# Delta rule's triangular inverse in 64x64 squares for tile 0, in whole width for tiles 1 and 2, with a new order on every engine

## What is computed

```python
kb = kc * bc[..., None]
lmat = jnp.where(strict, jnp.einsum('nbhid,nbhjd->nbhij', kb, kc) * decay, 0.0)
tmat = lax.linalg.triangular_solve(eye + lmat, eye, left_side=True, lower=True, unit_diagonal=True)
u = jnp.einsum('nbhij,nbhjd->nbhid', tmat, vc * bc[..., None])
```

```python
act = jnp.einsum('td,nd->tn', hf, expert_u)
a_sel = jnp.take_along_axis(act, eidx, axis=1)
coef = gates * jax.nn.gelu(a_sel, approximate=False)
dense = zeros.at[arange(T)[:, None], eidx].add(coef)
return dense @ expert_v
```

## Time and profile before

| | us |
|---|---|
| median of 3 runs | 1343.29 |
| lowest, highest | 1337.94, 1347.5 |
| the profiled execution | 1348.83 |
| its span (first to last instruction) | 1347.0 |
| granted TensorE clock, mean share | 0.861 |

### The profile page before, as it was taken

The page is one execution under the profiler, slowest core; times in us unless marked ns, Lnnn a source line. Parts: engine busy times, 40 slices in busy tenths (PEclk is TensorE's granted clock), DMA queues, the critical chain, the costliest instruction groups (busy, mean ns, idle before and its releaser), DMA issues.

```text
span 1347.0 us, 16598 instructions
## 1 busy us (share of the span) xinstructions
PE 902.6 (67%) x5942; PEld 510.0 (38%) x5942; DVE 859.9 (64%) x2283; ACT 265.2 (20%) x704; POOL 621.5 (46%) x660
## 2 busy tenths in 40 slices
PE   5896989979859877677860166001555877777775
PEld 2754668845525565354460022000112322322222
DVE  1624328899985598926199793898007766666565
ACT  3552414431314431304000001001001002000000
POOL 0010003236577556646667777776773433333330
PEclk9897989999969988889795578555787999999999
DMA  9664457999999789899999999999999999999995
GB/s 391 249 250 189 188 203 290 346 393 330 375 388 408 294 351 406 345 374 413 385 396 410 412 410 410 410 411 390 376 412 405 427 424 426 425 425 425 423 425 210
DMA packets 102305, 492.38 MB, mean 366 GB/s; under 512 B 11344, under 2 KB 12368, under 8 KB 80848
## 3 DMA queue, kind: packets, MB, share of 16 engines
q0 software_dynamic: 92624, 404.27, 75.0%
q1 hardware_dynamic: 9600, 87.05, 16.3%
HBM read 488.65 MB, written 2.62 MB: 365 GB/s over the span
## 4 chain that ended last, share of the span: by engine, by line
PE 35%; DMA 26%; DVE 20%; POOL 8%; issue 7%; ACT 4%; SPq 0%; DVEq 0%; POOLq 0%; ACTq 0%
PE bank L1202 32%; DMA big<-in_euv,consts 11%; DVE big L2033 9%; POOL big L800 6%; DMA wring<-in_euv,consts 5%; DMA wring<-in_wch 3%; DMA big<-in_ev,rowT 2%; DVE extra L2033 2%; PE bank L1222 1%; PE bank L1208 1%; DMA big<-in_eu,idx 1%; DVE wring L2033 1%; DMA extra<-in_eu,consts 1%; POOL extra L800 1%; DMA big<-in_eu,consts 1%
## 5 line engine op out<-in xcount | busy, mean ns | idle before, releaser
L1202 PE MATMUL bank<-big,W 128*32 128x512 f32 (+1 forms) x988 | 283.1, 725 | 103.0 <-DMA big<-in_ev,rowT 44.4
L2033 DVE CUSTOM_DVE_ANT_0 big<-big,hnow 128x1024 f32<-128x1024 f32 x240 | 284.7, 1217 | 103.3 <-DMA big<-in_euv,consts 51.5
L800 POOL DMA_INDIRECT big<-in_ev,rowT x171 | 163.2, 954 | 79.1 <-issue 59.2
L1202 PEld LDWEIGHTS bank<-big,W 128*32 128x32 f32 (+1 forms) x988 | 84.6, 148 | 258.5 <-issue 248.7
L1202 PE MATMUL bank<-hT,wring 128*128 128x128 f32 (+1 forms) x1088 | 152.4, 302 | 11.0 <-ACT hT L874 6.0
L1202 PE MATMUL bank<-wring,W 128*128 128x512 f32 (+1 forms) x352 | 126.5, 648 | 46.5 <-DVE W L2056 44.9
L1202 PEld LDWEIGHTS bank<-hT,wring 128*128 128x128 f32 x1088 | 143.6, 199 | 25.1 <-issue 12.5
L2033 DVE CUSTOM_DVE_ANT_0 wring<-wring,hnow 128x1024 f32<-128x1024 f32 x64 | 77.5, 1219 | 109.4 <-DMA wring<-in_euv,consts 109.2
L810 POOL DMA_INDIRECT big<-in_euv,consts x76 | 71.3, 939 | 102.0 <-PE bank L1202 98.5
L1202 PE MATMUL bank<-big 32*32 32x32 f32 (+1 forms) x1952 | 86.5, 228 | 42.3 <-issue 10.5
L789 POOL DMA_INDIRECT big<-in_eu,consts x102 | 96.6, 947 | 37.5 <-issue 24.4
(11 more groups left out here) (318 smaller groups left out, 1395.8 us busy)
## 6 DMA issues: line engine op xcount, KB each, us to landing
wring<-in_wch SPq DMA_DIRECT2D x32, 2048.0 KB, 10.8
big<-in_wch SPq DMA_DIRECT2D x6, 1536.0 KB, 9.3
tok<-in_wch SPq DMA_DIRECT2D x6, 512.0 KB, 10.4
big<-in_ev,rowT POOLq DMA_INDIRECT x171, 8.7
big<-in_eu,consts POOLq DMA_INDIRECT x102, 10.4
xs<-in_x SPq DMA_DIRECT2D x1, 1536.0 KB, 7.4
out_y<-xs SPq DMA_DIRECT2D x3, 512.0 KB, 7.8
big<-in_euv,consts POOLq DMA_INDIRECT x76, 17.8
```

Of the source, the lines that this page charges most:

```text
L800: nc.gpsimd.indirect_dma_start(row(slot), None, ev, bass.IndirectOffsetOnAxis(ap=rowT[t][:, n:n + 1], axis=0)).then_inc(rows_in[slot], 16)
L1202: return nc.tensor.matmul(out, lhsT, rhs, start=first, stop=last)
L2033: V.tensor_tensor_reduce(u, u, hnow[:, :], 1.0, 0.0, ALU.mult, ALU.add, coef[t % 2][:, n:n + 1]).then_inc(dot_ready, 1)
```

## The change

1. **Tile 0, levels 0 to 4** (`pi == 0`): `per_block` now makes two matmuls per head with a 64x64 stationary piece of a full-width matrix and 32 compact moving columns: 8 matmuls, 16 MATMUL records, instead of 16 and 32. L is masked to its 32x32 squares once (`LTB`). P comes out in compact form, DVE masks it and spreads it to 512 columns in one instruction (`in_blocks`). PE then forms TT (not T), DVE transposes it straight from PSUM to T, ACT copies TT. Level 0 is a product with a folded identity (`fold`, 32 more columns of constants), a mask and a transpose.
2. **Tiles 1 and 2**: all levels in whole width. Level 0 is one mask on 512 columns, 4 transposes on PE and one ACT copy. Levels 1 to 4 become what levels 5 and 6 were: 4 + 4 + 4 matmuls of 128x128, a mask on 512 columns, two ACT copies of 512 columns. The DVE transposes and `dn_full` are gone there.
3. **`grow` is gone**; the gate rows are made in `sq`, and each writer of `sq` waits, once, for the product that read the gate row (`sq_free`: in `rope`, `gate_rows`, `lam_step`, `head_norm`, `resid`, `take`). The masks grow from 960 to 1984 columns of 16 bits, 256 KB more to load.
4. **New lists** for all four engines. SP's list, the places of the rows and the order of the gathers among themselves are as before.

The core of the diff; the first `dn_t` is PE's, the second ACT's.

```diff
             def per_block(job, l, r):
                 for h in range(4):
                     c = slice(h * SB, (h + 1) * SB)
-                    for i in range(P // SB):
-                        q = slice(i * SB, (i + 1) * SB)
-                        ins = mm(b[q, c], l[q, c], r[q, c])
+                    for o in range(0, P, TB):
+                        q = slice(o, o + TB)
+                        ins = mm(b[q, c], l[q, h * P + o:h * P + o + TB], r[q, c] if r is not fold else r[q, :])
...
             def dn_p(t, d, lv):
-                if lv < SMALL:
-                    per_block(job, LTC[pi][d], TMC[pi][d])
+                if pi == 0 and lv < SMALL:
+                    per_block(("P", t, d, lv), LTB[pi][d], TMC[d])
                 else:
-                    per_head(job, [(LT[pi][d], TM[pi][d])])
+                    per_head(("P", t, d, lv), [(LT[pi][d], TM[pi][d])])
...
             def dn_t(t, d, lv):
-                if lv < SMALL:
-                    per_block(("T", t, d, lv), TTC[pi][d], PMC[pi][d])
+                if pi == 0 and lv < SMALL:
+                    per_block(("TT", t, d, lv), PM[pi][d], TTC[d])
                     return
                 if lv < LEVELS - 1:
                     per_head(("T", t, d, lv), [(TT[pi][d], PM[pi][d])])
...
             def dn_t(t, d, lv):
-                if lv < SMALL:
-                    evac(TMC[pi][d], ("T", t, d, lv), t_ready, ("T", t, d, lv), n=P)
+                if pi == 0 and lv < SMALL:
+                    act.wait_ge(*block_ready.at("T", t, d, lv))
+                    evac(TTC[d], ("TT", t, d, lv), t_ready, ("TT", t, d, lv), n=P)
                     return
...
             def dn_tt(t, d, lv):
-                dve.wait_ge(*t_ready.at("T", t, d, lv))
-                V.transpose(TTC[pi][d], TMC[pi][d]).then_inc(*block_ready.next("TT", t, d, lv))
+                job = ("TT", t, d, lv)
+                dve.wait_ge(*product.at(*job))
+                V.transpose(TMC[d], ps(*job)[:, 0:P]).then_inc(*block_ready.next("T", t, d, lv))
```

More of the change, by code:

```diff
@@ L188 @@
[L188 to L202, removed]
@@ new lines @@
+dn_t.0.0.3 dn_p.0.1.4 value.0.2 dn_p.0.0.4 dn_t.0.1.4 dn_t.0.0.4 mod.7 a_turn.0.3 dn_p.0.0.5 dn_p.0.1.5 dn_t.0.0.5
+dn_t.0.1.5 dn_p.0.0.6 dn_p.0.1.6 dn_t.0.0.6 dn_t.0.1.6 value.0.3 dn_v.0.0:2 dn_o.0.0:2 mod.8:10 gate.0.0.0 dn_s.0.0
+o_turn.0 gate.0.0.1 w_out.0.0 w_out_rest.0.0 w_out.0.1 w_out_rest.0.1 mod_turn.9 x_turn.1.0 dn_s.0.1 query.0.0
+query_rest.0.0 query.1.0 key_score.0.0 query_rest.1.0 channels.0.1 channels.1.1 channels.2.1 channels.3.1
+key_score.1.0 channels.4.1 c_turn.0.1 c_turn.1.1 channels.5.1 c_turn.2.1 channels.6.1 h_turn.0 channels.7.1 c_turn.3.1
@@ new lines @@
+c_turn.4.1 channels.8.1 channels.9.1 c_turn.5.1 channels.10.1 c_turn.6.1 channels.11.1 c_turn.7.1 query.2.0 c_turn.8.1
+query_rest.2.0 key_score.2.0 query.3.0 query_rest.3.0 c_turn.9.1 c_turn.10.1 c_turn.11.1 qk_turn.2 key_score.3.0
+mod.10:12 expert_rows.0.0 mod_turn.11 dn_decay.2.1 dn_scores.2.1 token.0.1:3 dn_t.2.1.0 dn_p.2.1.1 dn_t.2.1.1
+dn_p.2.1.2 dn_t.2.1.2 dn_p.2.1.3 token.2.1 dn_t.2.1.3 dn_p.2.1.4 dn_t.2.1.4 dn_p.2.1.5 qk_turn.1 dn_t.2.1.5 dn_p.2.1.6
+token.1.1 dn_t.2.1.6 token.1.2 dn_w.2.1 token.2.2 dn_v.2.1 dn_decay.1.0 dn_o.2.1 token.3.1:3 dn_scores.1.0 dn_s.2.1
@@ new lines @@
+dn_p.0.1.4 dn_p.0.0.4 dn_full.0.1 dn_full.0.0 dn_p.0.0.5 dn_p.0.1.5 dn_p.0.0.6 dn_p.0.1.6 head_norm.0.0 dn_o.0.0:2
+head_norm.0.1 gate.0.0.0 z_gate.0 dn_s.0.0 gate.0.0.1 resid.0.0:2 norm.1.0 mod_turn.9 scales.1 dn_s.0.1 top_key.0.0
+pair_sums.0.0.0 top_pair.0.0.0 places.0.0.0 chosen.0.0.0.0:2 channels.0.1 channels.1.1 experts.0.0.0 channels.2.1
+channels.3.1 top_key.1.0 channels.4.1 dot.0.0:2 channels.5.1 channels.6.1 channels.7.1 pair_sums.0.0.1 channels.8.1
+channels.9.1 channels.10.1 top_pair.0.0.1 dot.0.2:4 places.0.0.1 chosen.0.0.1.0 channels.11.1 key_norm dot.0.4
@@ new lines @@
+key_scale.2 key_scale.1 top_key.2.0 dot.0.5 chosen.0.0.1.1 dn_scale.2.1 dot.0.6 pair_sums.0.1.0 dot.0.7 experts.0.0.1
+expert_rows.0.0 dot.0.8:11 mod_turn.11 dn_decay.2.1 dot.0.11:13 dn_scores.2.1 dn_p.2.1.0 dot.0.13:15 dn_scale.1.0
+rope.1.0 top_key.3.0 dn_p.2.1.1 dot.0.15:18 dn_p.2.1.2 dot.0.18 dn_p.2.1.3 dot.0.19:26 pair_sums.0.1.1 dn_p.2.1.4
+dot.0.26:29 dn_p.2.1.5 dot.0.29:32 dn_p.2.1.6 dot.0.32:37 dn_qg.2.1 dot.0.37:45 top_pair.0.1.0 dot.0.45:48 rope.2.1
+dot.0.48:55 dn_decay.1.0 dot.0.55:59 places.0.1.0 dn_o.2.1 slot_gates.0.0 dn_scores.1.0 dn_s.2.1 chosen.0.1.0.0
@@ new lines @@
+dn_p.1.0.0 dot.0.59:63 dn_p.1.0.1 dot.0.63 coef.0.0 rope.2.0 top_pair.0.1.1 dn_scale.1.1 places.0.1.1 rope.1.1
+chosen.0.1.1.0 chosen.0.1.0.1 chosen.0.1.1.1 experts.0.1.0 dn_p.1.0.2 experts.0.1.1 slot_gates.0.1 expert_rows.0.1
+expo.1.0:2 diff.1.0 dn_p.1.0.3 dn_decay.1.1 dn_scores.1.1 dn_p.1.1.0 expo.1.2 diff.1.1 expo.1.3 diff.1.2 dn_p.1.0.4:6
+diff.1.3 dn_qg.1.1 dn_p.1.0.6 dn_p.1.1.1 dn_qg.1.0 head_norm.1.0 dn_o.1.0 dn_s.1.0 gate.0.1.0 expo.2.0 dn_scale.2.0
+dn_decay.2.0 dn_p.1.1.2 diff.2.0 dot.0.64:66 dn_scores.2.0 dot.0.66:69 dn_p.1.1.3 expo.2.1 dot.0.69 diff.2.1
```

316 lines of the change are left out of this document (159 added, 157 removed).

## The result

The changed kernel takes 1360.55 us (median of 4, 1358.06 to 1368.9) where the kernel before takes 1342.32 us beside it: ratio 1.0145, 95% interval 1.0088 to 1.0202. In a later comparison on like terms (run f1) the ratio is 1.0090, interval 1.0059 to 1.0121. So it is slower, by 12 to 18 us, where I had forecast no change. (A ratio is the comparison's own estimate and can differ from that of the medians by some 0.3%; both intervals lie above 1.) The busy times fit the edit: PE rises from 902.6 to 929.8 us, ACT from 265.2 to 283.1, DVE falls from 859.9 to 857.7. A second trace of each kernel has PE at 892.6 and 937.9 us, so a PE total is good to some 10 us.

The account below looks back on a forecast made before the run. It took DMA and POOL's gather issues plus gaps to bound the kernel behind 212 us. Terms -2.7, +2 and -3 gave -3.7 on 1348.83, 1345; less 5.5 to the median, 1340 us, range 1320 to 1364.

Parts of the forecast that it names:

- PE becomes the bound of 363 to 512 us: Rival: added PE work and longer chains delay all gathers there; +17 us, 1360 (1354 to 1372), chance 0.26.
- Stage by stage: Part pricing the delta rule of tiles 1 and 2 by pair and by POOL gap, +2 us in all.
- (1,0) and the start of (1,1): Added PE work before `v_batch.0.0.13`, PE idling 17.6 us in 363 to 400: +3 us, bounds -4 and +12.
- Gap of (1,1): POOL's 6.82 us wait at gather 160: levels 6 us longer but begun some 10 sooner: 0, bounds -5 and +10.
- the sum said +2: Tiles 1 and 2: +3 for (2,1), +3 for the batch, -4 for two thirds of the last gaps' total.
- the -3 behind 561 us: Gain from redone lists behind 561 us, not priced by rows: -3 us, bounds -6 and +6.
- PE +33 us for tiles 1 and 2: Whole-width products add 8.2 us of PE work per tile and direction, 33 for four.
- (2,1) +3, bounds 0 and 8: Stage 197 to 363 us: PE takes 8.2 us more, DVE gives 1.9 and gets `rope.2.1`; +3 us.
- Gap of the batch, +3: POOL's 9.29 us wait before 461 us for `v_batch.0.0.13` on PE grows: +3 us.
- Gap of dots, -6: POOL's 10.06 us wait before 500 us shrinks: a dot moves ahead and DVE has 3.8 us less; -6 us.
- Tile 0, -2.7: First part, up to the first gather at 212 us: fewer instruction stops, less added PE and DVE work; -2.7 us.
- The cover of 25 us at tile 1's indices: Indices ready at 635.27, used at 660.21 us: later delta rule of tiles 1 and 2 costs nothing that way.

Follow-up runs that it names:

- f1: The changed kernel unaltered, measured again beside its variants: 1355.60 us, 1.0090 of the kernel before.
- h2: Kernel before with tile 0 changed, plus whole width in tile 1's pairs (1,0) and (1,1) only, old order behind tile 0: 1360.20 us, 1.0115.
- f2: Changed kernel with the order of the kernel before behind about 545 us: 1352.10 us, 1.0060 of the kernel before.
- g1: Kernel before with tile 0 alone changed (64x64 squares, new order up to `dn_s.0.1`): 1343.68 us, 0.9986.
- g2: Changed kernel's products in all tiles, new order only up to `dn_s.0.1`, order of the kernel before behind it: 1364.90 us, 1.0169.
- g3: Changed kernel with the old order behind 545 us and whole-width products of levels 1 to 4, tiles 1 and 2, issued twice: 1378.96 us, 1.0283.
- i1: Kernel before with tile 0 alone changed, attention scores of tiles 1 and 2 issued three times: 1513.08 us, 1.0080, at the slower level.
- e2: Changed kernel with the order of the kernel before behind about 545 us, at the slower level: 1481.38 us, 0.9862 of the kernel before.
- e4: Kernel before with tile 0 alone changed (64x64 squares, new order up to `dn_s.0.1`), at the slower level: 1501.09 us, 0.9998.
- h1: Kernel before with tile 0 changed, plus whole width in the pair (2,1) only, old order behind tile 0: 1349.61 us, 1.0040.
- g4: The kernel before, unaltered, run for a second trace: 1342.45 us, one execution.
- h4: Changed kernel with each 64x64 product of tile 0 issued twice: 1362.67 us, 1.0123 of the kernel before.
- f3: Changed kernel with dots 116 to 127 ahead of `resid.2` on DVE and `s_copy.0.1` earlier on ACT: 1360.10 us, 1.0114 of the kernel before.
- f4: f3 plus an edit of PE's list, v-row batches 8 to 11 ahead of `query.0.2`: 1366.12 us, 1.0186 of the kernel before.

## Why the prediction was wrong

It said 1340 us and no change; it is 12 to 18 us slower. The wide range, 1320 to 1364, held the time only because it spanned most of the rivals too. The end that came is the one I had priced at 1360 as the rival "PE becomes the bound of 363 to 512 us".

**The step that failed** is in "Stage by stage": "(1,0) and the start of (1,1), +8.2 and +4, before `v_batch.0.0.13`: PE idles 17.6 us in 363 to 400 but mostly before its work is ready [...] +3", and "Gap of (1,1): [...] 0", with the reason against the rival, "POOL ran on until 447.15 without a stop". Whole width in tile 1 cost 17 us in the old order (h2) where these two terms said 3. The stop-free run of POOL showed only that PE was just in time: PE was busy 45.25 of 48.00 us in 400 to 448, so it had little room. The row was there; I read it as evidence for the rival and gave it 0.26. With the list that came with the change, what (2,1), the batch, the dots and (1,1) cost together is f2 against g1: 0.7%, 10 us with an interval of 5 either way, where the sum said +2. Of the miss of some 15 us (+12 in f1 for -3.7) that is 8; 6 or 7 are the -3 behind 561 us, a term without a row, where f1 less f2 is +3.5.

That more work for PE costs time is shown (g2, g3, i1). By which waits, and how much of it the longer chain of a level adds, is not. Nor does the account hold at the slower level, where whole width with the new list (e2) was faster than small squares with the old one (e4).

**Point by point.**

- *PE +33 us for tiles 1 and 2.* Right to a quarter: g2's PE total is 25.0 us above g1's (934.4 less 909.4), which differs by whole width and its steps alone. The 27.2 between the first two traces hold tile 0's part as well.
- *(2,1) +3, bounds 0 and 8.* 7 (h1, 2 to 12), inside the bounds.
- *Gap of the batch, +3.* Wrong in sign as a gap: 9.29 us at gather 131 became 0.30, with 2.81 at gather 127. The stretch from gather 64 to 127 grew all the same, from 82.1 and 80.4 us to 90.6 and 92.3. A price for one gap didn't price the stretch.
- *Gap of (1,1), 0.* 6.82 us ahead of gather 159 (5.49 in g4) became 3.67 (3.69 in f1); in the old order with whole width (g2) it stands at 6.93.
- *Gap of dots, -6.* Wrong in sign: it is 7.73 us in g4, 10.06 in the earlier trace rows, and 11.91 to 11.96 in the traces of the changed kernel, though the stretch that holds it, gather 127 to 160, got shorter (58.3 and 58.5 us for 62.1 and 67.0). I counted the dot that moves ahead and DVE's saved work, and nothing of what DVE waits for from PE.
- *Behind 561 us, -3, without a row.* Wrong in sign if anything: f1 less f2 is +3.5 us, inside the intervals. No run shows a gain there; an unpriced credit to "lists redone" should have been 0 with both bounds.
- *Tile 0, -2.7.* -1.8 (g1), with an interval from -5 to +2 that holds it. Its parts were other than I said. The stops of 8.9 us are gone and `w_out.0.0` starts at 156.45, as foretold (157). A 64x64 record costs (1.12 - 0.66) / 16 = 29 ns (foretold 30). `top_key.0.0` came 3.5 us earlier and `experts.0.0.0` behind two `channels` gave 4 back. But the gain hangs on TensorE's clock, which I didn't look at, though PEclk 0.60 stands in the earlier trace rows: see the last section.
- *The cover of 25 us at tile 1's indices.* Held: that they are written later cost nothing. It covered the wrong path.
- *The base.* I took the sum against one execution, 5.5 us above the median, and subtracted 5.5 at the end. The excess wasn't spread evenly: against g4 2.7 us of it lay ahead of gather 127 and 4.8 between 127 and 160, in the very gaps that I priced.

By the Trainium skill, "Runtime: NRT & Kernel Launch", Instruction fetch mechanics, crossing from one block of 256 instructions to the next is mostly hidden. By that rule fewer instructions would have given nothing. The doubled run (h4) agrees with it, with no stop by "issue" of 1 us in 576 small records; the three traces with 32x32 squares have 8.7 to 8.9 us of such stops each, and don't agree if these are fetches, which no run shows. The time doesn't decide it: the 7 us saved at `w_out.0.0` were worth 2 at the end.

The whole account at the level of the result, each from its run: tile 0 -2, whole width +21 to +25, new list up to 545 us -13 to -15, new list behind it +3 or nothing; with the +3 that is +9 by the medians and +12 by the ratios, against +12 measured for f1 and an interval of ±4.

## What to carry to other kernels

When an engine is busy 94% of a stage, don't take it for free that it hasn't made the next one wait yet: price added work there at a good part of its length (here 0.6 to 1.1 us per us), and count room only where a wait stands that is not the chain's. The longest stop in a trace need not be the loss; follow the same events through both kernels and see where the difference grows, in several executions of each: the same stretch of 96 gathers took 142.5 and 149.1 us in two traces of one kernel, and the effect looked for was 10. A hand-made order belongs to the durations it was made for: moved to other durations it cost about as much as it had gained, and mending one list of four gained nothing (f3) or lost (f4).
